# Gated recurrence of a two-block transformer: exponentials of summed log gates replaced by running products of the gates, half-width level products, and the output norm placed behind the next product's first tiles

## What is computed

```
f = lb + (1 - lb) * sigmoid(f_logit);  key = 1 - f;  qf = silu(q);  vf = i
att[t, s] = sum_k qf[t, k] * key[s, k] * prod_{s < r <= t} f[r, k]     (s <= t)
o[t] = sum_s att[t, s] * vf[s]
o = o * rsqrt(mean(o*o) + EPS) * norm_gain * silu(g)                     (per head and token)
mixed = concat([rmsnorm(attn), o]) @ w_out                               (2048 x 2048)
```

## Time and profile before

| | |
|---|---|
| median of 3 runs | 3144.05 us (3143.49 to 3147.2) |
| the profiled execution's own time | 3138.86 us |
| its span, first to last instruction | 3137.1 us |
| PE busy | 2789.2 us (89%) |
| DVE busy | 1936.0 us (62%) |
| ACT busy | 1282.1 us (41%) |
| mean granted TensorE clock | 0.946 of full speed |

### The profile page before, as it was taken

The page is one execution under the profiler, slowest core; times in us unless marked ns, Lnnn a source line. Parts: engine busy times, 40 slices in busy tenths (PEclk is TensorE's granted clock), DMA queues, the critical chain, the costliest instruction groups (busy, mean ns, idle before and its releaser), DMA issues.

```text
span 3137.1 us, 46257 instructions
## 1 busy us (share of the span) xinstructions
PE 2789.2 (89%) x19782; PEld 2430.0 (77%) x19782; DVE 1936.0 (62%) x2531; ACT 1282.1 (41%) x1738; POOL 113.4 (4%) x145
## 2 busy tenths in 40 slices
PE   2388996898988999999999999997699999999998
PEld 2367885787877888888888888777588888888887
DVE  4877663766754577667667655556745646565564
ACT  1133343323214555445435544445345434344343
POOL 0121101111100000000000000000000000000000
PEclk9989996989988899999999999998898999999998
DMA  8646661322215366667665545432053555555552
GB/s 321 247 162 212 216 215 40 114 84 98 86 65 191 104 200 203 228 201 231 216 197 175 182 142 160 151 128 83 14 189 129 182 187 187 188 188 188 185 184 88
DMA packets 287246, 514.64 MB, mean 164 GB/s; under 512 B 10048, under 2 KB 118592, under 8 KB 286912
## 3 DMA queue, kind: packets, MB, share of 16 engines
q1 hardware_dynamic: 283904, 500.21, 47.9%
q0 software_dynamic: 2704, 8.39, 0.8%
q10 hardware_dynamic: 432, 3.07, 0.3%
HBM read 509.40 MB, written 2.10 MB: 163 GB/s over the span
## 4 chain that ended last, share of the span: by engine, by line
PE 79%; DVE 11%; ACT 6%; issue 3%; DMA 1%; DVEq 0%; POOL 0%; ACTq 0%
PE ps L668 42%; PE ps L670 21%; DVE ACCa L1487 3%; PE ps L620 2%; DVE WLb L1504 1%; PE ps L807 1%; PE ps L802 1%; PE ps L792 1%; ACT WHb L1063 1%; PE ps L1004 1%; PE ps L695 1%; PE ps L606 1%; PE ps L959 1%; DVE MX L1568 1%; PE ps L759 1%
## 5 line engine op out<-in xcount | busy, mean ns | idle before, releaser
L668 PE MATMUL ps<-XB,WHb 128*128 128x512 f32 x2304 | 835.2, 405 | 35.8 <-DVE WLb L1504 18.9
L670 PE MATMUL ps<-XB,WLb 128*128 128x256 f32 x2304 | 650.3, 282 | 0.0
L1504 DVE TENSOR_TENSOR WLb<-RAWb,WHb 128x2048 fp32r<-128x2048 f32 (+1 forms) x196 | 427.0, 2192 | 329.9 <-ACT WHb L1063 329.7
L668 PEld LDWEIGHTS ps<-XB,WHb 128*128 128x128 f32 x2304 | 440.0, 191 | 145.1 <-issue 16.2
L1504 DVE TENSOR_TENSOR WLd<-RAWd,WHd 128x2048 fp32r<-128x2048 f32 x144 | 328.3, 2291 | 322.5 <-ACT WHd L1063 322.5
L1063 ACT ACTIVATE WHb<-RAWb 128x2048 fp32r<-128x2048 f32 (+1 forms) x196 | 356.8, 1833 | 321.2 <-PE ps L670 319.4
L668 PE MATMUL ps<-XD,WHd 128*128 128x512 f32 x1280 | 459.8, 403 | 12.2 <-DVE WLd L1504 12.2
L670 PEld LDWEIGHTS ps<-XB,WLb 128*128 128x128 f32 x2304 | 441.9, 192 | 0.5
L1063 ACT ACTIVATE WHd<-RAWd 128x2048 fp32r<-128x2048 f32 x144 | 274.1, 1914 | 358.9 <-PE ps L670 358.9
L668 PE MATMUL ps<-FB,WHd 128*128 128x512 f32 x1024 | 362.4, 399 | 0.0
L670 PE MATMUL ps<-XD,WLd 128*128 128x256 f32 x1280 | 361.0, 282 | 0.0
(11 more groups left out here) (313 smaller groups left out, 3628.1 us busy)
## 6 DMA issues: line engine op xcount, KB each, us to landing
RAWb<-in_ffn_w_in SPq DMA_DIRECT2D x168, 512.0 KB, 5.0
RAWd<-in_w_up SPq DMA_DIRECT2D x64, 1024.0 KB, 5.3
RAWd<-in_w_down SPq DMA_DIRECT2D x64, 1024.0 KB, 5.1
RAWa<-in_ada_w SPq DMA_DIRECT2D x48, 1024.0 KB, 5.1
RAWa<-in_rwkv_w_rkv SPq DMA_DIRECT2D x48, 1024.0 KB, 5.3
RAWb<-in_ffn_w_out SPq DMA_DIRECT2D x36, 1024.0 KB, 5.2
RAWs<-in_ada_w SPq DMA_DIRECT2D x32, 1024.0 KB, 5.1
RAWb<-in_w_in SPq DMA_DIRECT2D x24, 1024.0 KB, 5.0
```

What stands on the lines that cost most here:

```text
L668: pe.matmul(bank[:, :], WH[tag][:, w, o:o + P], acts(k), start=(k == 0), stop=False)
L670: mm = pe.matmul(bank[:, 0:T], WL[tag][:, w, o:o + P], acts(k)[:, 0:T], start=False, stop=last)
L1504: dve.tensor_tensor(WL[tag][:, n % WN, 0:size], RAW[tag][:, slot, 0:size], WH[tag][:, n % WN, 0:size].bitcast(F32), ALU.subtract).then_inc ...
```

## The change

- No logarithm, running sum or exponential. Levels go from small to large. `FQ` = q * f and `KY` = 1 - f are the queries and keys of level 0 (half-block 1). `ends[n]` holds for each block of 2^n tokens the product of its gates. From level n-1 to n (`update` on VectorE, h = 2^(n-1)), the second half of each pair of blocks in the queries is multiplied by the first block's end product, the first half of the keys by the second block's; the other halves are copied by ScalarE (`copies`). Queries and keys alternate between two buffers each (`FQ`/`QR`, `KY`/`FR_`).
- At each level only the second halves are streamed as queries: 16 products of 128 x 128 by 64 columns into two banks (`level`). The results of levels 0 to 4 are copied under a mask by VectorE (2 times 512), those of 5 and 6 by ScalarE as plain blocks; level 7 (h = 128) as before, 8 products.
- The products for s = t are multiplied by the identity (VectorE) in place of a memset of `AM` and a masked copy.
- The silu of `GR` moves from the head of `hgrn()` into the last group of `g_p`; the projection's column order and the slots in `PJ` are rearranged so that g is ready for it. The sums of squares for attention's norm move from ahead of `hgrn()` to behind level 1.
- Outputs use three banks; they are squared straight from the bank, and the gate multiply reads the bank.
- The barrier behind `hgrn()` goes. An unused stretch in the memory map (`clear_of_e`) keeps the weight rings clear of the recurrence's arrays: two chunks of `g_o2` are cast by ScalarE between its copies, a third after the root; VectorE makes the first low part after `update(7)`, the second after the inverse root. Attention's tiles are split inside `hgrn()`.
- The spread `b0` to `b3` is issued behind `g_o2`'s first two chunks (`beside_o2`); the final multiply and the split of tiles 8 to 15 follow. VectorE makes the low part of the third chunk after those.
- The mask array shrinks from 128 x 1024 to 128 x 320 words; `M128` goes.

```diff
-        p_tiles = [8, 9] + list(range(8)) + list(range(18, 26)) + list(range(10, 18)) + list(range(26, NP_))
+        p_tiles = [8, 9] + list(range(8)) + list(range(18, 26)) + list(range(10, 18)) + list(range(34, NP_))
+        p_tiles += list(range(26, 34))
...
+        sb(st_g, "clear_of_e", [P, 2576])
```

TensorE's list:

```diff
+                def level(n):
+                    h = 2 ** n
+                    if n:
+                        pe.wait_ge(*gV(0, f"k{n}"))
+                        pe.wait_ge(*gA(0, f"ck{n}"))
...
+                            for m in range(8):
+                                g = 8 * i + m
+                                z = slice((g % 2) * P, (g % 2) * P + P)
+                                q = queries[n % 2][:, g // 2, z].rearrange("p (b t) -> p b t", t=2 * h)[:, :, h:2 * h]
+                                mm = pe.matmul(bank[:, m * 64:(m + 1) * 64], keys[n % 2][:, g // 2, z], q, start=True,
+                                               stop=True)
...
+                level(0)
+                for g4 in range(4):
...
+                level(1)
+                last7[0] = (s_at, 8)
+                for j in range(8):
+                    stat("at", j, 8)
+                level(2)
+                level(3)
                 over_rows("at")
...
-                pe.wait_ge(*gV(0, "rc"))
-                for step in range(4):
...
+            def beside_o2():
...
+                    if g == 0 and ci == 1 and half:
+                        pe.wait_ge(*gV(0, "rc"))
+                        for step in range(4):
```

ScalarE's list in `hgrn()`:

```diff
+                for j in range(3):
                     square("at", j, PJ[:, j, :])
+                copies(1)
                 for g4 in range(4):
...
+                copies(2)
+                for j in range(3, 8):
+                    square("at", j, PJ[:, j, :])
+                copies(3)
                 root_only("at")
+                copies(4)
                 root_rows("at")
+                walk(g_o2.first)
+                copies(5)
+                walk(g_o2.first + 1)
+                copies(6)
```

VectorE's list in `hgrn()`:

```diff
+                def update(n):
+                    h, new, old = 2 ** (n - 1), n % 2, (n - 1) % 2
...
+                            dve.tensor_tensor(ends[n][:, :, None], end_of(n - 1, 0), end_of(n - 1, 1),
+                                              ALU.mult).then_inc(gV.sem, 1)
...
+                        dve.wait_ge(*gP(0, f"L{n - 2}_1"))
...
+                        dve.tensor_tensor(pairs(queries[new], h)[:, :, h:2 * h], pairs(queries[old], h)[:, :, h:2 * h],
+                                          end_of(n - 1, 0).to_broadcast([P, nb, h]), ALU.mult).then_inc(gV.sem, 1)
...
+                        dve.tensor_tensor(pairs(keys[new], h)[:, :, 0:h], pairs(keys[old], h)[:, :, 0:h],
+                                          end_of(n - 1, 1).to_broadcast([P, nb, h]), ALU.mult).then_inc(gV.sem, 1)
...
+                update(1)
+                dve.wait_ge(s_mk, 16)
+                for n in range(MASKED):
+                    masked(n)
+                    update(n + 2)
+                    if n == 1:
+                        root_mean("at", 1024)
+                    if n == 2:
+                        root_inverse("at")
                 dve.wait_ge(s_rst, rms_no["at"] + 1)
                 for j in range(4):
                     normed(j)
+                update(7)
+                walk(g_o2.first)
...
+                walk(g_o2.first + 1)
                 for step in range(4):
                     o = R[:, 8 + 2 * step:10 + 2 * step, :]
                     dve.wait_ge(*gP(0, f"b{step}"))
                     dve.wait_ge(*gV(0, f"og{step}"))
-                    dve.tensor_tensor(o, o, b2(banks[step]), ALU.mult)
+                    dve.tensor_tensor(o, o, b2(b_banks[step]), ALU.mult).then_inc(gV.sem, 1)
+                for j in range(8, ND):
+                    lo(j)
```

More of the change, by code:

```diff
@@ L27 @@
 WN = 3
-LEVELS = (64, 32, 16, 8, 4, 2, 1)
+MASKED = 5
 VEC_FIELDS = [
@@ L541, in two_blocks, with pairs, end_of, am_part @@
         bkv = BK[:, :, :].rearrange("p (g c) (s n) -> p g (c s) n", c=2, s=2)
-        QR, FR_, IR, GR = (PJ[:, 10 + 8 * n:18 + 8 * n, :] for n in range(4))
-        de1 = DE[:, 1, :].rearrange("p (j t) -> p j t", j=8)
+        IR, QR, FR_, GR = (PJ[:, 10 + 8 * n:18 + 8 * n, :] for n in range(4))
+        keys = [KY[:, :, :], FR_]
+        queries = [FQ[:, :, :], QR]
+        SQ = FQ[:, :, :].rearrange("p j t -> p (j t)")
+        ends = [FR_.rearrange("p j t -> p (j t)"), AU[:, :, :].rearrange("p j t -> p (j t)"),
+                PJ[:, 8:10, :].rearrange("p j t -> p (j t)"), EE[:, 0:256], EE[:, 256:384], EE[:, 384:448],
+                EE[:, 448:480]]
+        def pairs(x, h):
+            return x.rearrange("p j (b t) -> p (j b) t", t=2 * h)
+        def end_of(n, half):
+            e = ends[n].rearrange("p (b i) -> p b i", i=2)
+            return e[:, :, half:half + 1]
+        def am_part(i, h):
+            return AM[:, 8 * i:8 * i + 8, :].rearrange("p g (b t) -> p g b t", t=2 * h)[:, :, :, h:2 * h]
+        def l_part(name, h):
+            return g_bank(name).rearrange("p (g b t) -> p g b t", g=8, t=h)
+        first_banks = [tile_bank[g_o2.tile0 + t] for t in range(4)]
+        o_banks = [banks[b][:, :] for b in range(7) if b not in first_banks]
+        b_banks = o_banks + [banks[7][:, :]]
         f_uses = []
@@ L962, in hgrn @@
-                pe.wait_ge(*gA(0, "it3"))
-                pe.wait_ge(*gA(0, "L0_1"))
-                pe.wait_ge(*gV(0, "L7_3"))
+                level(0)
+                for g4 in range(4):
+                    bank = take(f"it{g4}")
+                    for m in range(4):
+                        g = 4 * g4 + m
+                        mm = pe.transpose(bank[:, m * P:(m + 1) * P], IR[:, g // 2, (g % 2) * P:(g % 2) * P + P],
+                                          ident)
+                    mm.then_inc(gP.sem, 1)
@@ L1336, in hgrn @@
-                for li, h in levels[2:]:
-                    exps(li, h)
+                walk(g_o2.first)
+                copies(5)
+                walk(g_o2.first + 1)
+                copies(6)
+                act.wait_ge(*gV(0, f"L{MASKED - 1}_1"))
+                for i in range(2):
+                    part = g_bank(f"L5_{i}").rearrange("p (g t) -> p g t", t=64)
+                    g8 = slice(8 * i, 8 * i + 8)
+                    act.wait_ge(*gP(0, f"L5_{i}"))
+                    act.activation(AM[0:32, g8, 32:64], part[0:32, :, 0:32], ACT.Copy)
+                    act.activation(AM[64:96, g8, 96:128], part[64:96, :, 32:64], ACT.Copy).then_inc(gA.sem, 1)
@@ new lines, in hgrn @@
+                copies(7)
+                for j in range(4):
+                    gained(j)
+                for i in range(2):
+                    part = g_bank(f"L6_{i}").rearrange("p (g t) -> p g t", t=64)
+                    act.wait_ge(*gP(0, f"L6_{i}"))
+                    act.activation(AM[0:64, 8 * i:8 * i + 8, 64:128], part[0:64, :, :], ACT.Copy).then_inc(gA.sem, 1)
+                for i in range(2):
+                    act.wait_ge(*gP(0, f"L7_{i}"))
+                    act.activation(AU[:, 4 * i:4 * i + 4, :], b4(g_bank(f"L7_{i}")), ACT.Copy).then_inc(gA.sem, 1)
@@ L1434, in scalar_program @@
             hgrn()
-            barrier(act, tally)
             lim = g_m[-1][1].end
-            for j in range(ND):
-                act.activation(XD[:, j, 0:T], R[:, j, :], ACT.Copy).then_inc(s_xh, 1)
             gemm(g_o2, lim, evac_to(to_r), squared_behind("o2", g_o2, 3))
```

320 lines of the change are left out of this document (162 added, 158 removed).

## The result

The changed kernel takes 3118.95 us (median of 6 runs, 3113.2 to 3128.09); in the same rounds the kernel before took 3143.77 us (median of 6). The ratio is 0.9928, 95% interval 0.9904 to 0.9952: faster by 25 us, inside the stated range of 3092 to 3126, 16 us slower than the point forecast of 3103 and 7 us above the band given to the forecast itself (3095 to 3112). The profiled execution took 3113.2 us, its span is 3111.4 us.

The account below looks back on a forecast made before the run. VectorE was taken to bound the levels (busy 52.60 of 59.3 us). The stretch behind the barrier, 81.4 + 1.4 + 1.6 = 84.4 against 125.8 us, gave 41 less: 3098 profiled, 3103 as median, range 3092 to 3126.

Parts of the forecast that it names:

- The load sets it and not the columns: TensorE in the levels: weight load sets record spacing, so half-width products save nothing and a level keeps 3.7 us.
- 46.5 us for 404 records: TensorE's records from the barrier to the last sum of squares, at 0.115 us each.
- a fifth of the following 52 us (costs 4.7): After the first 8 us behind the barrier, a fifth of the time at 1.2 GHz, costing 4.7 us.
- The term for the first 8 us (3.3): Start behind the barrier: TensorE's first 8 us run at 1.2 GHz, costing 3.3 us.
- the clock stays at 0.5: Sign of being wrong, from barrier to last sum: granted clock at 0.5 instead of 0.85 to 0.9.
- the clock staying low through the levels: Rival: all 404 records at 0.202 us, 112 us for the stretch, 14 less, 3130 us; chance 0.13.
- The full-clock rival: Full clock throughout the stretch, no slow restart: 74.8 us, 51 less, 3093 us; chance 0.12.
- the standstill: Behind the spread, TensorE idles 6.2 us for final multiply, low parts, gate copy and chunk 2's `WL`.
- the restart: Chunk 2 starts at 1.2 GHz after TensorE's idle time, costing 1.6 us.
- no stride on TensorE: Slower rival: strided queries at levels 0 to 5 (192 records) cost TensorE; loss from 0.21 us more each; chance 0.03.
- The rival of levels in turns: Levels take turns instead of overlapping: 7.1 us each, 25 us less in all, 3119 us; chance 0.14.
- fine strides cost VectorE nothing: VectorE in the levels: strided operands add no time; a level takes 3.6 to 4.2 us instead of 7.0.

Follow-up runs that it names:

- four-bank control: Against the kernel streaming 128 columns at levels 0 to 6 in four banks: same banks, readers and order, only 64 columns streamed; 3128.02 us, one run.
- second timing: The changed kernel, unaltered, timed again beside the kernel before in five rounds: 3119.95 against 3139.7 us, ratio 0.9931 (0.9905 to 0.9957).

## Why the prediction came out as it did

**Right: what bounds a level.** "The load sets it and not the columns": 32 records of 64 columns took 3.69 us, of 128 columns in the same place 3.74. The 46.5 us for 404 records is therefore a fair estimate for a full clock. The Trainium skill, "TensorE: Matmul & The Clock Gate", section "Back-to-back issue gap", has an isolated gap that would be about half as long for 64 columns; it also says that in a stream weight load and product set the spacing together. By this pair the 64-column records take 99%, so the second statement is the one that fits here.

**Wrong in size: the clock.** The step that failed is "a fifth of the following 52 us (costs 4.7)". Of the time from the keys' instruction to the last sum, forecast 46.5 for records, 8.0 for the clock and 5.7 for waits, the profile has 5.19 + 12.40 + 38.26 + 10.95 = 66.8 us of busy TensorE and 70.5 - 66.8 = 3.7 of waits. So the clock cost 66.8 - 46.5 = 20.3 us, 12.3 more than the term. Levels 2 to 6, 6.8 us from start to start for 3.7, are 15.7 of it, the products for s = t another 1.6, the rest level 7, the spread over rows and part of the outputs. The term for the first 8 us (3.3) was too large, so the one for what follows was further off than the sum shows: 20.3 - 1.6 = 18.7 us for 4.7. Waits cost 2.0 less; 1.0 of that is the wait at level 5, which is gone because a slow TensorE gets there late enough. The last sum came at 70.5 instead of 60.2. The prediction's own signs say the same: levels 3.7 to 4.5 us apart and a granted clock of 0.85 to 0.9 up to the last sum were named, 6.8 (from level 2 on) and 0.69 were found, and "the clock stays at 0.5", named as a way to be wrong, is what levels 2 to 6 did. One reading behind the term is off as well: in the kernel before, the clock behind 2253.57 rose not 4.8 but 5.8 us into the products (0.50 up to 2259.0, 0.64 from there to 2259.5).

The argument behind the step was that "TensorE will be busier than now". Busier it is, and it did not help. The rival that named it, the clock staying low through the levels, had the right observation ("busy time alone doesn't raise it, and the new products have half the columns") and only 0.13. As a mechanism it holds for levels 2 to 6; its price of 14 us gained was too dark, since levels 0 and 1, most of the outputs and both chunks ran at the full clock. The full-clock rival is refuted: levels 2 to 7 were granted 0.52. The Trainium skill, "TensorE: Matmul & The Clock Gate", section "What's actually happening", has activity release the throttled state. The four-bank control does not bear that out for these products: 34.7 us of them without a gap left the clock at 0.50.

**Right: the end.** Chunks 0 and 1 took 11.3 us (forecast 11.3), the spread 3.73 (3.7), the standstill 5.7 (6.2), the restart 1.3 (1.6). What the forecast did not ask is whether this order is a good one: 6.9 us lay in the place of the spread, and up to 3.4 us in the split that stands ahead of the squares. The forecast had this wait in its sum (2.1 us for the first square) without asking what the order without it would be.

**Right: no turns, no stride on TensorE.** Strided queries cost TensorE nothing (level 0 at 3.69, 128 unstrided columns at 3.74; at the lower clock level 6, which has no stride, took 7.03 like the strided ones), and at the full clock levels 0 and 1 lie 5.3 us apart only because the transposes lie between. The rival of levels in turns priced its case at 7.1 us a level and 3119 us, and 3119 us with levels 6.8 us apart is what came out. That is a coincidence: in turns TensorE would have been idle for nearly half of each level, and it was busy 38.26 of 39.00 us.

**Wrong: "fine strides cost VectorE nothing".** It holds for the multiplies (1.21 to 1.22 us at every level of the changed kernel), not for the masked copies: two at levels 0 and 1 took 2.5 and 2.4 us, where the forecast had 1.3. A level of VectorE was 5.3 and 4.9 us there instead of at most 4.2, more than TensorE's 3.7. In the changed kernel this cost TensorE no wait, since transposes and sums stand behind these levels; where the sums were moved away TensorE waited 0.90 us for VectorE, and the clock fell behind that pause. At the full clock, with no other work between them, VectorE would by these rows have held back the small levels; that is an estimate, and no run shows it beyond this one pause.

**Not foreseen: a loss elsewhere.** In the stretch the forecast was 41 us and the traces show 31.5: 9.5 us are the clock less the small terms. That part of the miss is explained by the runs; the rest is not. The other 7 us of the miss (12 by the second timing) come from outside it. By the profiled executions alone: 32.9 less in the stretch, 8.6 more ahead of it, 1.4 less behind, together 25.7, which is 3138.86 - 3113.2.

## What to carry to other kernels

Halving the columns of a float32 product behind a full weight load, 128 to 64, saved TensorE nothing here (3.69 us for 3.74), and once the clock was down behind such products, one-column sums or a pause, 64-column products never got it back: they ran at half the clock for as long as they lasted. When the bound moves from VectorE to TensorE, look at the granted clock of the stages with similar products, not at how busy TensorE will be. And when work is put behind the next product's first tiles, leave one chunk behind it as well: something must cover the chain that it sets off.

## What was not expected of the hardware

- TensorE busy 34.70 of 34.70 us with 64-column float32 products was granted 0.50 throughout, while 128-column products in the same banks and order were back at the full clock within one level (5.28 us, then 3.74). In the changed kernel, two unused records of 256 columns ahead of each 16 of 64 columns did not bring the clock back either.
- The same 64-column products kept the full clock for three levels when they followed 128-column products without a gap, and lost it in the level behind a pause of 0.90 us (4.58, then 6.93). With 128 columns a pause of 0.64 us cost nothing (3.81). The two pauses were not tried with the other's columns.
- Behind the same standstill of 5.7 us, one kernel lost 1.3 us in one profile and 2.8 us in another before chunk 2 ran at the full clock.
- Two masked copies of 512 elements took VectorE 2.5 us where the runs that they write are 1 or 2 elements long (levels 0 and 1); one took 0.7 us where the runs are 4 or more.
